# Attention slots of the second mixer: mask first, then values, scores, and the transposes last

## The reference, cut to what matters

```python
def masked_softmax(s, mask):
    s = jnp.where(mask, s.astype(jnp.float32), -jnp.inf)
    m = jnp.max(s, axis=-1, keepdims=True)
    m = jnp.where(jnp.isfinite(m), m, 0.0)
    e = jnp.exp(s - m)
    den = jnp.sum(e, axis=-1, keepdims=True)
    return e / jnp.where(den > 0, den, 1.0)
...
        return gg[..., 0:1] * o_c + gg[..., 1:2] * o_s + gg[..., 2:3] * o_w
```

## Time and profile before

| what | value |
|---|---|
| median of 3 runs | 903.11 us (903.11 to 903.37) |
| span of the profiled execution, first to last instruction | 901.3 us |
| the profiled execution's own time | not listed; the median is 1.8 us above its span |
| PE busy | 893.6 us, 99% of the span |
| DVE busy | 624.8 us, 69% |
| ACT busy | 504.8 us, 56% |
| DMA | 155.27 MB, mean 172 GB/s |
| attention slots 0 to 13 | from 513.8 us (first scores) to 620 us |

### The profile page before, as it was taken

How to read it: one execution, slowest core, us unless ns; L and a number is a source line. 1 busy time by engine, 2 the same in 40 slices (tenths; PEclk the granted TensorE clock), 3 DMA queues, 4 the chain that set the end, 5 groups by cost and what they waited for, 6 DMA issues and landing times.

```text
span 901.3 us, 12594 instructions
## 1 busy us (share of the span) xinstructions
PE 893.6 (99%) x4946; PEld 761.6 (85%) x4946; DVE 624.8 (69%) x793; ACT 504.8 (56%) x701; POOL 79.0 (9%) x145
## 2 busy tenths in 40 slices
PE   9999999999999999999999999999999999999998
PEld 7888878887889888888889988777888888888887
DVE  5646566765876566666585898998887595666664
ACT  6646655545355444444466878977464564444441
POOL 8603342130010000000000000000000000000000
PEclk9999999999999999999999999999999999999999
DMA  8654333466554655555545764443446376556551
GB/s 274 222 187 152 128 102 121 152 225 220 184 157 156 218 187 186 186 186 187 187 141 186 236 189 139 134 131 112 139 147 209 111 233 191 185 190 201 182 170 47
DMA packets 103380, 155.27 MB, mean 172 GB/s; under 512 B 2650, under 2 KB 70338, under 8 KB 103331
## 3 DMA queue, kind: packets, MB, share of 16 engines
q1 hardware_dynamic: 102416, 151.57, 51.6%
q0 software_dynamic: 864, 2.98, 1.0%
q10 hardware_dynamic: 50, 0.04, 0.0%
HBM read 153.53 MB, written 1.05 MB: 172 GB/s over the span
## 4 chain that ended last, share of the span: by engine, by line
PE 96%; ACT 1%; issue 1%; POOL 0%; DMA 0%; DVE 0%; POOLq 0%; ACTq 0%; DVEq 0%
PE PS L628 19%; PE PS L630 19%; PE PS L629 19%; PE PS L1017 15%; PE PS L1022 8%; PE PS L681 3%; PE PS L687 1%; PE PS L907 1%; PE PS L1153 1%; PE PS L1131 1%; PE PS L1065 1%; PE PS L1189 1%; PE PS L894 0%; PE PS L858 0%; DMA res<-in_x_dram 0%
## 5 line engine op out<-in xcount | busy, mean ns | idle before, releaser
L1937 DVE TENSOR_TENSOR wlo<-raw,whi 128x2048 fp32r<-128x2048 f32 x141 | 324.2, 2301 | 124.0 <-ACT whi L1341 122.3
L1341 ACT CAST whi<-raw 128x2048 fp32r<-128x2048 f32 x141 | 269.2, 1909 | 112.1 <-PE PS L630 109.2
L1017 PE MATMUL PS<-hT,whi 128*128 128x512 f32 x608 | 144.7, 390 | 0.0
L1017 PEld LDWEIGHTS PS<-hT,whi 128*128 128x128 f32 x608 | 113.2, 188 | 23.2 <-issue 0.2
L628 PE MATMUL PS<-whi,hT 128*128 128x512 f32 (+1 forms) x320 | 126.2, 395 | 0.0
L630 PE MATMUL PS<-whi,hT 128*128 128x512 f32 (+1 forms) x320 | 123.1, 385 | 0.0
L629 PE MATMUL PS<-wlo,hT 128*128 128x512 f32 (+1 forms) x320 | 122.9, 384 | 0.0
L628 PE MATMUL PS<-whi,aT_hi 128*128 128x512 f32 x216 | 84.3, 391 | 0.0
L629 PE MATMUL PS<-wlo,aT_hi 128*128 128x512 f32 x216 | 84.3, 390 | 0.0
L630 PE MATMUL PS<-whi,aT_lo 128*128 128x512 f32 x216 | 84.0, 389 | 0.0
L1022 PEld LDWEIGHTS PS<-hT,wlo 128*128 128x128 f32 x608 | 78.0, 191 | 3.0
(11 more groups left out here) (385 smaller groups left out, 1303.5 us busy)
## 6 DMA issues: line engine op xcount, KB each, us to landing
raw<-in_w_in_dram SPq DMA_DIRECT2D x47, 1024.0 KB, 5.1
raw<-in_w_ff_dram SPq DMA_DIRECT2D x32, 1024.0 KB, 5.5
raw<-in_w_gate_dram SPq DMA_DIRECT2D x11, 1024.0 KB, 5.3
raw<-in_w_up_dram SPq DMA_DIRECT2D x11, 1024.0 KB, 5.3
raw<-in_w_down_dram SPq DMA_DIRECT2D x11, 1024.0 KB, 5.0
raw<-in_w_out_dram SPq DMA_DIRECT2D x8, 1024.0 KB, 5.0
raw<-in_w_proj_gla_dram SPq DMA_DIRECT2D x4, 1024.0 KB, 6.6
raw<-in_w_mem_kv_dram SPq DMA_DIRECT2D x4, 1024.0 KB, 5.0
```

The source lines that it names most:

```text
L1017: pe.matmul(PS[:, bank + c, :], w_hi[:, k, c * P:(c + 1) * P], hT[:, k, :, :].rearrange("p w t -> p (w t)"), start=k == 0, stop=False, ski ...
L1341: act.copy(whi[:, n % RING, :], raw[:, n % RING, :]).then_inc(hi_made, 1)
L1937: dve.tensor_tensor(wlo[:, n % RING, :], raw[:, n % RING, :], whi[:, n % RING, :].bitcast(F32), ALU.subtract).then_inc(lo_made, 1)
```

## The change

att_scores is split in two. A new att_mask(i) carries the wait for att_e and, for unit 0, the one for the mask tile; it issues the two mask matmuls, which now open the two banks (start=True). For a memory unit it only waits. att_scores(i) adds the scores onto that (start=False). In a step the order on PE becomes att_mask(i), att_values(i - 3), att_scores(i), att_turn(i - 2). The number and the shapes of the instructions stay as they are, and so does every other engine's program. att_s is now added to by the last score matmul instead of the last mask matmul.

```diff
--- before.py
+++ after.py
@@ -1101,13 +1101,27 @@
                                            start=True, stop=True)
                 mm.then_inc(fn_sum, 1)
 
-            def att_scores(i):
+            def att_mask(i):
+
                 kind, a, g = ATT[i]
                 if i >= 1:
                     pe.wait_ge(att_e, 4 * i)
                 if i == 0:
+                    pe.wait_ge(maskr_made, 1)
+                if kind == "m":
+                    return
+                L = 15 if kind == "c" else P * (a + 1)
+                m = mask_r[:, P + 30 * a:P + 30 * a + 30] if kind == "c" else mask_r[:, 0:P].unsqueeze(1).to_broadcast([P, 2, P])
+                for e in range(2):
+                    z = PS[:, e, 0:2 * L]
+                    if kind != "c":
+                        z = z.rearrange("p (h n) -> p h n", h=2)[:, :, P * a:P * a + P]
+                    pe.matmul(z, ident_r[:, :], m, start=True, stop=False, skip_group_check=True)
+
+            def att_scores(i):
+                kind, a, g = ATT[i]
+                if i == 0:
                     pe.wait_ge(kd_made, 1)
-                    pe.wait_ge(maskr_made, 1)
                 if i in (0, 1):
                     c = f"q{i}"
                     pe.wait_ge(drained[unit_of[c] % 2], unit_of[c] // 2 + 1)
@@ -1128,14 +1142,8 @@
 
                     L = 15 if kind == "c" else P * (a + 1)
                     k = kcT[r, 15 * g:15 * g + 15] if kind == "c" else kdup[kind][r, g, 0:L]
-                    pe.matmul(PS[:, h % 2, h // 2 * L:(h // 2 + 1) * L], q, k, start=h < 2, stop=False, skip_group_check=True)
-                if kind != "m":
-                    m = mask_r[:, P + 30 * a:P + 30 * a + 30] if kind == "c" else mask_r[:, 0:P].unsqueeze(1).to_broadcast([P, 2, P])
-                    for e in range(2):
-                        z = PS[:, e, 0:2 * L]
-                        if kind != "c":
-                            z = z.rearrange("p (h n) -> p h n", h=2)[:, :, P * a:P * a + P]
-                        mm = pe.matmul(z, ident_r[:, :], m, start=False, stop=True, skip_group_check=True)
+                    mm = pe.matmul(PS[:, h % 2, h // 2 * L:(h // 2 + 1) * L], q, k, start=False, stop=h >= 2,
+                                   skip_group_check=True)
                 mm.then_inc(att_s, 1)
 
             def att_turn(i):
@@ -1261,12 +1269,14 @@
                                            w2v[:, f, :], start=f == 0, stop=f == 1)
                     mm.then_inc(kc_sum, 1)
                 i = s - ATT_AT - 3
+                if 0 <= s - ATT_AT < len(ATT):
+                    att_mask(s - ATT_AT)
                 if 0 <= i < len(ATT) and (ATT[i][0] == "m" or i % 2 == 1):
                     att_values(i)
+                if 0 <= s - ATT_AT < len(ATT):
+                    att_scores(s - ATT_AT)
                 if 0 <= s - ATT_AT - 2 < len(ATT):
                     att_turn(s - ATT_AT - 2)
-                if 0 <= s - ATT_AT < len(ATT):
-                    att_scores(s - ATT_AT)
                 if s == 25:
                     pe.wait_ge(att_lo, 6)
                     pe.wait_ge(taps, 124)
```

## The result

The changed kernel takes 904.37 us (median of 21 runs, 904.06 to 904.83) against 903.21 for the kernel before (median of 21 runs beside it). The ratio is 1.0014, with a 95% interval of 1.0008 to 1.0020: slower by 0.7 to 1.8 us. The interval leaves out 1, so the loss is real, but it lies inside the 0.2% that the prediction counted as no change. The forecast was 904.6 us from 903.11, +1.5 us; the medians differ by 1.16, the two profiled spans by 1.7.

The account below looks back on a forecast made before the run. TensorE (PE), busy 893.6 of 901.3 us, was taken as the bound; 0.57 + 0.90 + 0.21 - 0.40 + 0.21 = +1.5 us on 903.11 gave 904.6 us, with an 8-in-10 range of 902.9 to 906.1.

Parts of the forecast that it names:

- case A: The forecast itself: exponentials end later than PE's projection in slots 2, 8 and 9, giving 904.6 us; chance 0.62.
- step 1: Mask's wait for ACT's exponentials, no longer behind values and transposes: +0.57 in slot 2, +0.90 in 8, +0.21 in 9.
- the release in slot 2 doesn't move: Unit 1's exponentials, begun behind the maximum, end when they did; extra cost of slots 0 and 1 disappears in slot 2's wait.
- step 2: Joins between narrow and full matmul forms on PE: -0.40 over slots 4, 6, 8, 10; +0.21 over seven other slots.
- Rival B: ACT's exponentials move with PE: slot 9 stalls 1.01, slot 10 0.76, +1.6 more, 906.1 us; chance 0.16.
- Rival C: Earlier scores bring the exponentials forward, hiding the waits; only joins and slots 0 and 1 count, 903.1 us; chance 0.12.
- Rival D: Each change of shape on PE costs a drained matmul: -1.1 for -0.4, 903.9 us with stalls, 902.2 without; chance 0.10.
- Who is served later: DVE gets scores sooner, ACT's copy gets transposes up to 1.1 us later, about 1.7 in slot 12; all costs 0.

Follow-up runs that it names:

- mask-third run: Against the kernel before: order values, transposes, mask, scores, so the mask opens the bank and the scores come last; PE +0.77 us behind slot 13.
- with one copy: Changed kernel with ACT's copy of unit 5's transposes made once more, awaited; shift behind slot 13 +3.38 us against the kernel before.
- with two: Changed kernel with ACT's copy of unit 5's transposes made two more times, each awaited; shift behind slot 13 +3.96 us against the kernel before.

## Why the prediction was right

The forecast of +1.5 us met +1.16 by the medians and +1.35 by the trace, and case A was the one that came. The stalls were right; that the sum is so close is partly luck, since the steps up to slot 2 were 0.14 too low and the changes of shape 0.27 too high. Point by point, by its own steps:

- **The wait loses its cover** (step 1): right in all three places. Idle ahead of the mask 1.26, 0.90 and 0.20 us, forecast about 1.2, 0.90 and 0.21; slot 10 free, by 0.5 instead of 0.3. The orders with values first and with one slot alone show that it is the cover, and that each part stands by itself: 0.59 for slot 2 alone, 0.79 for slot 8 alone. Making ACT shorter or longer moved these idle times. One link was used without being said for slot 8: its stall was worked out as if slot 2 had cost nothing, which is right only because ACT, too, came 0.40 later there.
- **That the release in slot 2 doesn't move, and that slots 0 and 1 vanish in it**: wrong by 0.12 (the forecast for slots 0 to 2 was 0.57, measured 0.71). The exponentials of unit 1 ended 525.38 - 513.32 = 12.06 behind the query sums, before 524.85 - 512.91 = 11.94. The prediction hung them on the maximum alone. That was ready only 0.03 later (523.34 - 513.32 = 10.02, before 522.90 - 512.91 = 9.99), but ACT's own cast and copies stand ahead of them too, and this row of work waits for PE to end the projection behind slot 0: it starts at 521.14 - 513.32 = 7.82, before at 520.61 - 512.91 = 7.70, so 0.12 later. Slot 2 alone gives 0.59, all of the changed kernel up to there 0.71.
- **Changes of shape** (step 2): the sum for the value slots was -0.40, measured 0.19 + 0.03 + 0.18 in slots 4, 6 and 10, and 0.90 - 0.82 = 0.08 in slot 8: -0.48. That one change fewer is worth 0.10 everywhere didn't hold: it was worth 0.18 and 0.19 where the scores have 15 columns and the mask 30 (slots 4 and 10), 0.03 and 0.08 where both are wide (slots 6 and 8). By the reading of the mask-third run, a mask of 30 columns is too short to hide the weight loads behind it, so moving it away costs nothing there; this is argued and not shown. The other slots, taken at +0.03 each, +0.21 in all, gave 0.00, -0.09, +0.01, +0.03, -0.03, +0.10 and 0.00 in slots 3, 5, 7, 9, 11, 12 and 13: +0.02. With 0.71 for slots 0 to 2, the sum is 0.71 + 0.90 + 0.20 - 0.48 + 0.02 = 1.35.
- **Rival B** (ACT moves with PE): fell. Slot 10 has no idle time and slot 9 only 0.20. ACT followed PE's 0.4 from before slot 8, but not the 0.9 of slot 8.
- **Rival C** (waits hidden): fell for the changed kernel, and the run with values first shows the one form in which half of it holds: slot 8's wait is hidden there and comes back in slot 9.
- **Rival D** (a change costs a whole matmul): fell. It wanted 0.3 less in each slot with values; none gained more than 0.19.
- **Who is served later**: right that it costs nothing. ACT's wait for transposes rose from 0.2 to 2.1 us and nothing followed from it. DVE's wait at the maximum of slot 8 shrank from 1.02 to 0.52, not to 0.8, as DVE's own work ahead of it also came later.

The Trainium skill's sentence that a change of tiling mode drains TensorE (TensorEngine Tiling, Key Properties) agrees with the joins of 0.09, but a join is not the whole price in this kernel: in the mask-third run the number of changes is that of the kernel before, and 0.77 us are lost all the same.

## What to carry to other kernels

When an instruction that waits is moved forward in a queue, write down for each round when its releaser ends and when the engine would now arrive; the difference is the stall, and it is paid once per lateness, not once per round, as long as the other engine doesn't follow. Where it does follow, as ACT did between slots 2 and 8, the lateness covers nothing later and the next stall is paid in full. Do this against the kernel that you change, not against the trace of another order: a round that is free there may be free only because the engine is late. Put work that needs nothing (here the values) ahead of the wait, and join pieces of one shape, but expect tenths of a microsecond from the latter and a microsecond from the former.

## What was not expected of the hardware

PE's idle time has a second price. In the changed kernel it is 1.26 us at most and the granted clock stays full; with 1.5 us in slot 2 it did so in ten runs of ten. With 1.5 and 2.1 us of idle time in slot 8, one execution each, the clock fell to its lower level 1.4 us after the mask with one copy (578.4 against 576.98) and 2.6 us after it with two (579.5 against 576.94), stayed there for 3.4 us, and cost 1.6 us beyond the idle time itself, 1.4 of it at the end. In slot 2, with 1.9 us, four runs of ten show a lower mean clock (0.998) and 1.4 to 2.1 us more than the median of the other six. What tells the executions apart stays open.
